# Hymba encoder layer: raw tokens are projected, each token's root is applied later

## What is computed

```python
h = rmsnorm(x, norm_g)                       # x * rsqrt(mean(x*x) + 1e-6) * norm_g
z = h @ w_in                                 # 2272 columns, split among the groups
o_mla  = latent attention of c_q, c_kv, k_rope   (c_q, c_kv normed again, 4 heads)
o_pool = (windowed means of u minus u) @ w_pool * pool_scale
o_gla  = rmsnorm(gated linear attention of q, k, v, decay gates; forward + backward)
x = x + concat(o_mla*silu(gate), o_pool*silu(gate), o_gla*silu(gate)) @ w_out
y = rmsnorm(x, final_norm_g)
```

## Time and profile before

| | us |
|---|---|
| median of three runs (797.66 to 800.98) | 799.07 |
| the profiled execution | 801.39 |
| its span | 799.60 |
| busy: TensorE products, weight loads | 762.3, 639.3 |
| busy: DVE, ACT, POOL | 402.6, 322.9, 213.4 |

### The profile page before, as it was taken

One profiled execution on the slowest core, in us unless ns is written; L12 is line 12 of the kernel. 1 busy time (PEld: TensorE's weight loads), 2 busy tenths in 40 slices (PEclk: granted clock), 3 DMA queues, 4 the chain that ended last, 5 costly groups with the idle time before them and its releaser, 6 DMA issues.

```text
span 799.6 us, 14673 instructions
## 1 busy us (share of the span) xinstructions
PE 762.3 (95%) x6092; PEld 639.3 (80%) x6092; DVE 402.6 (50%) x699; ACT 322.9 (40%) x566; POOL 213.4 (27%) x251
## 2 busy tenths in 40 slices
PE   5999999999999999999998899999999989999996
PEld 3997878877888887888886788888888878788884
DVE  3653796265565521026164566666666762532332
ACT  4551625443355532432223545444545452323221
POOL 3223216444456321232400000000008513333220
PEclk8899999999999999999999999999999999999999
DMA  6412021100112113330133000000024024644541
GB/s 241 136 57 73 27 91 53 28 29 28 68 59 90 67 61 104 116 93 27 60 145 119 4 21 18 14 14 14 14 69 196 1 83 142 198 152 146 173 144 52
DMA packets 40045, 64.53 MB, mean 81 GB/s; under 512 B 4241, under 2 KB 23089, under 8 KB 39985
## 3 DMA queue, kind: packets, MB, share of 16 engines
q1 hardware_dynamic: 33984, 49.51, 19.1%
q10 hardware_dynamic: 6000, 14.16, 4.6%
HBM read 44.00 MB, written 19.27 MB: 79 GB/s over the span
## 4 chain that ended last, share of the span: by engine, by line
PE 76%; DVE 12%; ACT 5%; issue 5%; DMA 2%; POOL 0%; SPq 0%; POOLq 0%; ACTq 0%; DVEq 0%
PE psum L78 21%; PE psum L80 20%; PE psum L79 20%; DVE a_top L1782 4%; DVE a_turned_lo L1809 3%; PE psum L1301 2%; PE psum L1847 2%; PE psum L1323 2%; ACT a_turned_hi L1759 1%; PE psum L1192 1%; ACT a_weights L1739 1%; DMA n_x_in<-in_x_dram 1%; PE psum L1366 1%; PE psum L1839 1%; PE psum L1838 1%
## 5 line engine op out<-in xcount | busy, mean ns | idle before, releaser
L78 PE MATMUL psum<-h_hi,z_w_hi 128*128 128x512 f32 (+1 forms) x480 | 183.9, 383 | 0.0
L80 PE MATMUL psum<-h_hi,z_w_lo 128*128 128x512 f32 (+1 forms) x480 | 177.9, 371 | 0.2 <-issue 0.2
L79 PE MATMUL psum<-h_lo,z_w_hi 128*128 128x512 f32 (+1 forms) x480 | 177.7, 370 | 0.0
L78 PEld LDWEIGHTS psum<-h_hi,z_w_hi 128*128 128x128 f32 x480 | 91.4, 190 | 17.8 <-issue 2.2
L80 PEld LDWEIGHTS psum<-h_hi,z_w_lo 128*128 128x128 f32 x480 | 91.3, 190 | 16.2 <-issue 0.6
L79 PEld LDWEIGHTS psum<-h_lo,z_w_hi 128*128 128x128 f32 x480 | 91.5, 191 | 14.5 <-issue 0.7
L1739 ACT ACTIVATE a_weights<-psum,a_bias,mla_q_scale 128x1024 f32<-128x1024 f32 (+1 forms) x48 | 51.1, 1064 | 105.4 <-DVE a_bias L1785 105.4
L78 PE MATMUL psum<-o_w_hi,o_m_hi 128*128 128x512 f32 x192 | 75.9, 395 | 2.0 <-DVE o_m_lo L2053 1.7
L80 PE MATMUL psum<-o_w_hi,o_m_lo 128*128 128x512 f32 x192 | 75.5, 393 | 0.0
L79 PE MATMUL psum<-o_w_lo,o_m_hi 128*128 128x512 f32 x192 | 75.3, 392 | 0.0
L1809 DVE TENSOR_TENSOR a_turned_lo<-psum,a_turned_hi 128x512 fp32r<-128x512 f32 x80 | 52.2, 687 | 41.7 <-ACT a_turned_hi L1759 41.7
(11 more groups left out here) (219 smaller groups left out, 1464.2 us busy)
## 6 DMA issues: line engine op xcount, KB each, us to landing
z_w_raw<-in_w_z_dram SPq DMA_DIRECT2D x17, 512.0 KB, 3.5
n_x_in<-in_x_dram SPq DMA_DIRECT2D x12, 512.0 KB, 3.9
gates_scratch<-z_gate ACTq DMA_DIRECT2D x24, 256.0 KB, 2.0
o_x_in<-in_x_dram SPq DMA_DIRECT2D x12, 512.0 KB, 3.6
out_dram<-o_y ACTq DMA_DIRECT2D x12, 512.0 KB, 3.2
o_w_raw<-in_w_out_dram SPq DMA_DIRECT2D x8, 512.0 KB, 9.3
rope_scratch<-p_rope_split SPq DMA_DIRECT2D x12, 256.0 KB, 2.7
a_q_rope<-rope_scratch SPq DMA_DIRECT2D x48, 64.0 KB, 1.9
```

Source lines behind the costliest of these rows:

```text
L78: nc.tensor.matmul(out, a_hi, b_hi, start=first, stop=False)
L79: nc.tensor.matmul(out, a_hi, b_lo, start=False, stop=False)
L80: return nc.tensor.matmul(out, a_lo, b_hi, start=False, stop=last)
```

## The change

Tokens are transposed as they come, 256 at a time (a unit), in quarters of two channel tiles each (four transposes). The norm weights, turned into a column, scale the copies `h_hi` and `h_lo`. The squares are taken from the raw tokens after their turn. The per-token reciprocal root no longer meets `h`: it is turned into rows (`turn_rstd`, `copy_rstd`) and multiplied into the first nine blocks when DVE empties them (`empty_scaled`; ACT's `empty` now begins at block 9). Queries and keys stay unscaled, values get the squared root as ACT takes them, the latents' and the linear attention's own norms carry it in their epsilon, and the gates are multiplied by it when they are read again, from a ninth plane of the gate memory. Block 0 is multiplied in two halves of 256 tokens with turns inside, blocks 1 and 3 have a turn after each channel tile, and blocks 2, 4 and 5 run with 512 columns. The core of the diff, indentation cut:

```diff
 def load_x(n):
     if n >= X_SLOTS:
-        sp.wait_ge(norm_ready, n - X_SLOTS + 1)
-    sp.dma_start(x_in[:, n % X_SLOTS, :], dram["x"][n * P:(n + 1) * P, :]).then_inc(x_loaded[n % X_SLOTS], 16)
+        sp.wait_ge(squares_done, 2 * (n - X_SLOTS) + 2)
+    sp.dma_start(x_in[n % X_SLOTS][:, :, :], dram["x"][unit_tokens(n), :].rearrange("(a p) d -> p a d", a=2))\
+      .then_inc(x_loaded[n % X_SLOTS], 16)
...
+sp.dma_start(ident[:, :], dram["ident"]).then_inc(ident_loaded, 16)
+load_w(0)
 load_x(0)
-sp.dma_start(ident[:, :], dram["ident"]).then_inc(ident_loaded, 16)
-sp.dma_start(g_row[:, :], dram["norm_g"].partition_broadcast(P)).then_inc(g_loaded, 16)
 load_x(1)
-load_w(0)
-load_x(2)
 load_w(1)
-load_x(3)
-for n in range(X_SLOTS, TILES):
+for n in range(2, UNITS):
     load_x(n)
+load_w(2)
 sp.dma_start(gate_up[4 * GATE_RANK:6 * GATE_RANK, :, :], dram["gate_up"]).then_inc(early_loaded, 16)
...
 sp.dma_start(pool_scale[:, :], dram["pool_scale"]).then_inc(early_loaded, 16)
-load_w(2)
-sp.wait_ge(z_emptied, 5)
+sp.wait_ge(rstd_copied, TB)
+sp.dma_start(gates_dram[POWER_PLANE, :, :], rstd_rows[:, :]).then_inc(rstd_stored, 16)
+sp.wait_ge(z_scaled, 5)
...
 def square(n):
-    act.wait_ge(x_loaded[n % X_SLOTS], 16 * (n // X_SLOTS) + 16)
-    if n >= 2:
-        act.wait_ge(turned, 2 * n - 2)
-    nc.scalar.activation(x_norm[:, n % 2, :], x_in[:, n % X_SLOTS, :], ACT.Square, scale=D_MODEL ** -0.5,
-                         accum_out=mean_sq[:, n:n + 1]).then_inc(squares_done, 1)
+    u = n // 2
+    act.wait_ge(turned, QUARTERS * (u + 1))
+    nc.scalar.activation(x_in[u % X_SLOTS][:, n % 2, :], x_in[u % X_SLOTS][:, n % 2, :], ACT.Square,
+                         scale=D_MODEL ** -0.5, accum_out=mean_sq[:, n:n + 1]).then_inc(squares_done, 1)

 def take_hi(n):
-    for half in range(2):
-        act.wait_ge(turned, 2 * n + half + 1)
-        nc.scalar.activation(h_hi[:, 4 * half:4 * half + 4, n * P:(n + 1) * P],
-                             psum[:, 6 + half, :].rearrange("p (k t) -> p k t", k=4),
-                             ACT.Copy).then_inc(hi_ready, 1)
+    u, k0 = n // QUARTERS, 2 * (n % QUARTERS)
+    act.wait_ge(turned, n + 1)
+    for k in (k0, k0 + 1):
+        ins = nc.scalar.activation(h_hi[:, k, unit_tokens(u)], psum[:, 6 + n % 2, (k - k0) * UNIT:(k - k0 + 1) * UNIT],
+                                   ACT.Copy, scale=g_column[:, k:k + 1])
+    ins.then_inc(hi_ready, 1)
...
+act.dma_start(g_rows[0:KT, :], dram["norm_g"].rearrange("(k p) -> k p", p=P)).then_inc(g_loaded, 16)
...
+for n in range(2 * QUARTERS):
+    take_hi(n)
+split_hi(1)
 square(0)
 square(1)
...
+for n in range(2 * QUARTERS, 4 * QUARTERS):
     take_hi(n)
-    if n + 2 < TILES:
-        square(n + 2)
-for i in range(EARLY):
-    empty(i)
-    if i == 4:
-        split_hi(2)
+for n in range(2, 8):
+    square(n)
+for n in range(4 * QUARTERS, 6 * QUARTERS):
+    take_hi(n)
+for n in range(8, TILES):
+    square(n)
+split_hi(2)
...
-    empty(i)
+    if i >= SCALED:
+        empty(i)
...
+split_lo(0)
+split_lo(1)
+for b in range(TB):
+    invert_powers(b)
...
-    pool.wait_ge(z_emptied, TB * (u + 2))
+    pool.wait_ge(z_scaled, TB * (u + 2))
...
 def take_lo(n):
-    for half in range(2):
-        dve.wait_ge(hi_ready, 2 * n + half + 1)
-        at = (slice(None), slice(4 * half, 4 * half + 4), slice(n * P, (n + 1) * P))
-        nc.vector.tensor_tensor(h_lo[at], psum[:, 6 + half, :].rearrange("p (k t) -> p k t", k=4),
-                                h_hi[at].bitcast(F32), ALU.subtract).then_inc(lo_ready, 1)
+    u, k0 = n // QUARTERS, 2 * (n % QUARTERS)
+    dve.wait_ge(hi_ready, n + 1)
+    for k in (k0, k0 + 1):
+        ins = nc.vector.scalar_tensor_tensor(out=h_lo[:, k, unit_tokens(u)],
+                                             in0=psum[:, 6 + n % 2, (k - k0) * UNIT:(k - k0 + 1) * UNIT],
+                                             scalar=g_column[:, k:k + 1], in1=h_hi[:, k, unit_tokens(u)].bitcast(F32),
+                                             op0=ALU.mult, op1=ALU.subtract)
+    ins.then_inc(lo_ready, 1)
+
+def copy_rstd(b):
+    dve.wait_ge(rstd_mm, b + 1)
+    nc.vector.tensor_copy(rstd_rows[:, b * BLK:(b + 1) * BLK], psum[:, 6 + b % 2, :]).then_inc(rstd_copied, 1)
+
+def empty_scaled(i):
+    o, tb = EARLY_BLOCKS[i] if i < EARLY else (i // TB, i % TB)
+    t = slice(tb * BLK, (tb + 1) * BLK)
+    dve.wait_ge(z_done, i + 1)
+    dve.wait_ge(rstd_copied, tb + 1)
+    if i == EARLY:
+        dve.wait_ge(rstd_stored, 16)
+    nc.vector.tensor_tensor(z[:, ORDER[o], t], psum[:, bank_of(i), :], rstd_rows[:, t], ALU.mult).then_inc(z_scaled, 1)
...
-dve.wait_ge(g_loaded, 16)
...
+nc.vector.tensor_copy(g_column[:, :], psum[:, 7, 0:KT]).then_inc(g_copied, 1)
+dve.wait_ge(g_copied, 1)
...
     take_lo(n)
+copy_rstd(0)
+empty_scaled(0)
+empty_scaled(1)
+for n in range(4 * QUARTERS, 6 * QUARTERS):
+    take_lo(n)
+copy_rstd(1)
+empty_scaled(2)
+empty_scaled(3)
+copy_rstd(2)
+empty_scaled(4)
+empty_scaled(5)
 dve.wait_ge(early_loaded, 16 * EARLY_CONSTS)
-for n in range(2 * TB):
+add_bias(0)
+add_bias(1)
+empty_scaled(EARLY)
+for n in range(2, 2 * TB):
     add_bias(n)
+empty_scaled(EARLY + 1)
 pool_windows(0)
+empty_scaled(EARLY + 2)
 pool_windows(1)
 add_up_gates(FWD)
...
 def turn(n):
...
+        pe.wait_ge(g_copied, 1)
+    if n >= 2:
+        pe.wait_ge(lo_ready, n - 1)
+    if n == 4 * QUARTERS:
+        pe.wait_ge(rstd_copied, 1)
+    for k in (k0, k0 + 1):
+        for a in range(2):
+            at = (k - k0) * UNIT + a * P
+            mm = nc.tensor.transpose(psum[:, 6 + n % 2, at:at + P], x_in[u % X_SLOTS][:, a, k * P:(k + 1) * P], ident[:, :])
+    mm.then_inc(turned, 1)
...
-        if i >= EARLY:
-            pe.wait_ge(z_emptied, 1 if i == EARLY else 2 if i == EARLY + 1 else i - 1)
+        if i in (EARLY, EARLY + 1):
+            pe.wait_ge(z_scaled, i - EARLY + 1)
+        elif EARLY + 1 < i <= SCALED + 1:
+            pe.wait_ge(z_scaled, i - 1)
+        elif i > SCALED + 1:
+            pe.wait_ge(z_emptied, i - 1 - SCALED)
...
+def project_unit(u):
+    pe.wait_ge(w_lo_ready, 1)
     for k in range(KT):
+        if k % 2 == 0:
+            pe.wait_ge(lo_ready, QUARTERS * u + k // 2 + 1)
         c = slice(k * P, (k + 1) * P)
-        mm = product(nc, psum[:, i, part * UNIT:(part + 1) * UNIT], w_hi[:, o, c], w_lo[:, o, c],
-                     h_hi[:, k, t], h_lo[:, k, t], k == 0, k == KT - 1)
-    if part:
+        mm = product(nc, psum[:, 0, u * UNIT:(u + 1) * UNIT], w_hi[:, 0, c], w_lo[:, 0, c],
+                     h_hi[:, k, unit_tokens(u)], h_lo[:, k, unit_tokens(u)], k == 0, k == KT - 1)
+        if k in (1, 3):
+            turn(QUARTERS * u + k // 2 + 2)
+        if u == 0 and k >= 6:
+            turn(QUARTERS + k - 6)
+    if u:
         mm.then_inc(z_done, 1)
...
+def project_turning(i, first_turn):
+    for k in range(KT):
+        project(i, k, k + 1)
+        turn(first_turn + k)
...
-keep_running(14)
-pe.wait_ge(ident_loaded, 16)
-for n in range(3):
-    turn(n)
-    if n < 2:
-        keep_running(5)
-for j in range(2 * EARLY):
-    project_early(j)
-    if j + 3 < TILES:
-        turn(j + 3)
+keep_running(6)
+turn_g()
+keep_running(6)
+turn(0)
+turn(1)
+project_unit(0)
+project_unit(1)
+project_turning(1, 2 * QUARTERS)
+pe.wait_ge(lo_ready, 4 * QUARTERS)
+project(2, 0, KT)
+turn_rstd(0)
+project_turning(3, 4 * QUARTERS)
+pe.wait_ge(lo_ready, 6 * QUARTERS)
+project(4, 0, 4)
+turn_rstd(1)
+project(4, 4, KT)
+project(5, 0, 4)
+turn_rstd(2)
+project(5, 4, KT)
...
+    if m == FIRST_GATE_STEP:
+        scale_first_gate()
...
-finish(0, 0, True)
-take_hi(1, 0, False)
-store(0, 0)
-finish(0, 1, True)
-take_hi(1, 1, False)
-store(0, 1)
+    finish(0, s, True)
+    take_hi(1, s, False)
+    store(0, s)
...
+def scale_gate(i, s):
+    dve.wait_ge(gate_loaded[s], 16 * i + 16)
+    nc.vector.tensor_tensor(gate[s][:, 0:KT, :], gate[s][:, 0:KT, :], gate[s][:, KT:KT + 1, :].broadcast_to([P, KT, P]),
+                            ALU.mult).then_inc(gate_scaled, 1)
...
 take_lo(0, 0)
+scale_gate(0, 1)
```

237 lines of the change are left out of this document (123 added, 114 removed).

## The result

The changed kernel took **823.48 us** (median of four, 821.67 to 825.52), the kernel before 798.97 us beside it: a ratio of 1.029, 95% interval 1.027 to 1.032. It is slower, as forecast, but by 24.5 us and not by 5.8; the range ended at 810. The profiled execution took 821.67 us, span 819.80, so 20.2 us of span have to be found.

A forecast was written before the change was run, and what follows sets the result against it. TensorE, fed late and slow-clocked at the start, then DVE's chain to windows(1), bound the kernel; +5.4 us at the pool heads and +0.4 later made +5.8 on the 799.07 median: 804.9 us, range 799 to 810.

The forecast's parts named there:

- steps 1 to 5: Start to end of block 5: first product 9.7, TensorE work 45.0, waits 9.1, slow clock 1.9, sum 65.7 us.
- B: The mark at the end of block 5: 65.3 us in the profiled kernel before, 65.7 us forecast.
- The clock term: Start: one slow stretch of about 5 us at clock 0.50, costing 1.9 us, bounds 0 and 4.1.
- rival A: Start: no slow clock stretch, all else as forecast, block 5 ends at 63.8, total 803.0 us; chance 0.18.
- The early start is spent: At the end of block 5: the earlier first product gains nothing there, 65.7 against 65.3 us.
- Rival D: Start: hi/lo pairs overlap fully, TensorE never waits from 9.7 us, block 5 ends 54.7 to 56, total 794.5; chance 0.08.
- step 6: Block 5's end to pool heads: DVE's longer chain starts them at B+45.2, 110.9 us, 5.4 later than before.
- Nothing later catches up: After the pool heads: their 5.4 us delay stays, since TensorE's own work is unchanged to 400 us.
- step 7: Attention and output: one scaling on DVE costs 0.8 us (0 to 1.2), output gives back 0.4; net +0.4.
- Rival E: Exposed behind DVE: block 8's emptying late for block 10, or attention scaling at every step; 810 to 812; chance 0.06.
- Time that moves after 400 us: Attention and later: any time shift after 400 us would show the forecast wrong; no size given.
- its paragraph on the shared ports: At windows(1): shared SBUF port blocks the later of DVE and POOL; sum 2.1 us less if DVE is first.

The follow-up runs named there:

- c1_fillers: b3_all plus eleven unread products in TensorE's holes before the first turn and the first product; 799.54 us, ratio 0.9985.
- c3_before_heads: The kernel before with its three pool heads one block later; 799.46 us, ratio 0.9985.
- a1_gate_late: The changed kernel with the first gate scaled four steps of attention later; ratio 1.018, span 810.8 us.
- a2_gate_alone: The changed kernel with POOL's splits of the last two output weight slices waiting until the first gate is scaled; ratio 1.022, span 812.9 us.
- a3_windows_first: The changed kernel with DVE making windows(0) before it empties block 7; ratio 1.022, span 810.9 us.
- a4_heads_late: The changed kernel with the three pool heads and their evictions one block later; ratio 1.019, span 814.4 us.
- b3_all: b2_order with quarter turns issued earlier and the pool heads one block later; 800.63 us, ratio 0.999.
- b1_both: The changed kernel with the first gate scaled four steps later and windows(0) before the emptying of block 7; ratio 1.014, span 810.3 us.
- b2_order: b1_both with biases 2 and 3 before the emptying of block 6 and second weights split after the fourth hi pair; 804.60 us, ratio 1.005.

## Why the forecast had the sign and missed the size

**Start and products (steps 1 to 5): B at 65.7 forecast, 67.0 measured.** The whole is close, its terms less so. The first product came at 10.55 us, not 9.7 (tokens at 7.8, not 6.9, inside the bounds and near the 8 of its second estimate). Waits behind it are 8.2 us against 9.1: 1.50 for the second weights, not 1.9; 1.84 before blocks 2 and 4, as forecast at 1.9; 3.0 in the first block and at the first root turn, not 3.4. A hi pair took 0.84 and a lo pair 0.88 us, as priced. TensorE's own work was mis-sized: 67.0-10.55-8.2 = 48.2 us, not 45.0. A quarter turn between 512-column products costs 0.56 us, seven pitches of turn and product from 25.59 to 34.28 us less 0.68 each, not 0.48; that is 1.8 us if all 22 cost it (16 stand between such products). The other 1.4 us I could not assign to rows. The clock term (1.9) is 0 in this profile, and in four others block 5 ends 1.1 to 1.5 us later behind a low start: it comes in some executions and not in others, which neither the forecast nor rival A allowed for.

"The early start is spent" held, and more strongly than I put it: even with its joints mended and its clock kept (c1_fillers, 64.2) block 5 ends no earlier than in the kernel before when that is little disturbed (c3_before_heads, 62.8). Rival D was never near.

**After B (step 6): pool heads at B+48.7, not B+45.2.** The mechanism was right, bias stall 1.44 us (1.5) included. (From its B+28.9 the forecast's own terms make B+45.0, 0.2 less than it wrote.) Two sizes were wrong. windows(0) starts at B+21.1, not B+19.6, since block 7 ran 1.6 us of its time at the low clock behind that stall. Nine of ten profiles with the stall show this stretch between 80 and 88 us, none of the four without it. And windows(1) takes 16.5, not 14.45 us: I carried over the one lengthened addition of before, but not that shifting windows(1) by several microseconds lays its end beside POOL's next split, at 110.9 us. It ended at 105.47 before, ahead of that split. This is 2.0 us.

**"Nothing later catches up" was true; that nothing later is added was false.** TensorE waits 6.45 us at the pool heads, and 3.0 us of low clock follow. I had a clock term for the start, where the trace of before showed one, and none for the two waits that I forecast myself (1.5 and 4.5 us). This term was missing, 4.6 us with the 1.6 above in this profile; behind the same 6.45 us it was 1.4 in two others.

**Attention (step 7) is the step that failed: 0 to 1.2 us forecast, 7.7 measured.** I priced the scaling by its nearest row and took 0.8. With POOL out of its way that holds: its length is 1.22 us, and attention takes 0.8 and 0.9 us more than before in a1_gate_late and a2_gate_alone. What I did not look at was POOL's program beside the step at which it stands: back-to-back splits of the output weights until 644.1 us. a2_gate_alone shows that they alone make 6.57 us of 1.21. TensorE then stood 3.65 and 2.47 us, with 1.7 us of low clock behind. The trace of before had these rows, which neither the forecast nor its groups of rows show; there POOL was busy like this from 602.37 to 631.3 us:

```profile
627.68 1.16 POOL L1709 CAST o_w_hi<-o_w_raw 128x512 fp32r<-128x512 f32 x2
628.81 2.53 POOL L1714 TENSOR_TENSOR o_w_lo<-o_w_raw,o_w_hi 128x512 fp32r<-128x512 f32 x2
```

Rival E was the only one to name the scaling ("in attention at every step behind it", 810 to 812); the measured loss is one blocked instruction, and larger. "Time that moves after 400 us", which the forecast had named as a sign that it was wrong, is what came. The forecast held the mechanism in hand: its paragraph on the shared ports used the row of windows(1) (3.91 for 1.78 us). The Trainium skill (SBUF — State Buffer, "SBUF: two separate sides") says that of a DVE instruction with two SBUF inputs and a POOL instruction that reads SBUF the later one is fully blocked; the trace agrees at all three places, and the first gate's scaling is such an instruction. I weighed the rule at the one place where I already saw its effect, and not at the one that the change adds. By rule and rows, the wait for POOL is what is left of its queue, 644.1-638.6 = 5.5 us, plus 1.2: 6.7, against 6.57 measured. In a3_windows_first and a4_heads_late the same sum gives 7.3 and 7.4, against 7.15 and 7.29.

**Output (step 7): -0.4 forecast, -0.7 measured.** The eleven scalings are hidden there.

Of the 20.2 us, 6.9 are DVE's chain to the pool heads (5.0 forecast, 2.0 POOL's second split in it), 1.7 the start, 4.6 the clock behind two waits and 7.7 attention (0.8 forecast); the output phase gave back 0.7. The medians lie 24.5 us apart and the profiled spans 20.2, since the profiled execution of before was 2.4 us above its median and that of the change 1.8 below: the four executions fall into 821.7 and 821.9 at a mean clock of 0.986 and 0.984, and 825.0 and 825.5 at 0.978 and 0.983, so the profile of the change is of the shorter kind.

**Is there a version worth having?** b3_all takes back all 24 us by order alone, with no arithmetic changed, and ends at 0.999 of before; c1_fillers, with unread products added, at 0.9985. One edit of order to the kernel before gives the same 0.9985. The intervals of all three reach 1.000. No gain of the new arithmetic over the old can be shown.

## To carry to other kernels

- For every operation that a change adds to DVE with both inputs in SBUF, read POOL's timeline at that moment, and price it at what POOL's back-to-back instructions have left to run plus its own length; an operation of 1.2 us cost 7.7 with the waits and the clock behind it. Four steps later it took its own 1.22 us, and attention 0.8 us more than before.
- When a piece of work moves from an idle engine into the program of a busy one, the price is its place in the order, not its length: one emptying of 0.69 us ahead of windows(0) made DVE stand 6.5 us, and the next engine's wait grew from 1.1 to 6.45 us.
- A wait that you forecast on TensorE gets a second term for the clock behind it, here 1.6 us behind 1.44 and 1.4 to 3.0 behind 6.45. Where that term comes only in some executions, one profile is not the median.

## What the runs showed of the hardware

- A single DVE instruction was held out across the POOL instruction that ran and five more in a row (one split, two casts, two splits, 639.2 to 644.1 us), casts with one input among them; it did not get its turn between two. In a3_windows_first and a4_heads_late, where it met the queue earlier, it took 7.15 and 7.29 us.
- The granted clock fell to 0.50 with the waits of 6.45 us (four profiles) and 2.24 us (one) at the pool heads, not with those of 1.06 us or 0.61. The same wait of 6.45 us cost 3.0, 2.9, 1.4 and 1.4 us of low clock. Behind the stall of 1.44 us before block 7 it fell in nine of ten profiles, behind the 1.84 us before blocks 2 and 4 in three of 22 places (b1_both and b2_order), behind the start's holes of 0.5 to 2.0 us in six of twelve. What decides between these cases no run here shows.
- Unread products ahead of the pool heads kept the clock at 1.00 there in two profiles of two, and the pool heads came no later after block 5 (48.8 and 48.7 us, 48.7 without). In both, a hole of 1.7 to 1.95 us that no other profile has stood about 60 us later. In the start none of two profiles with them had the low stretch, which is too few to tell.
